# Stick-breaking heads taken in pairs with keys in chunks of 512, and a reordered expert loop

## The chip, the cores and the metric

One core of a Trainium2 chip runs the whole kernel. The metric is the device time in microseconds (us). Its engines are TensorE (PE, with weight loads as PEld), VectorE (DVE), ScalarE (ACT), GpSimd (POOL) and SyncE (SP); each runs its own program, and they meet only at semaphores.

## What is computed

An encoder block on 1024 tokens of width 1024, all in float32:

```python
h = rms_norm(x); q, k, v of both head groups = h @ w_in + b_in
# 8 stick-breaking heads of 64, no softmax; strict means key < query
log_1m  = where(strict, log_sigmoid(-z), 0)          # z = q k^T / 8
between = reversed cumsum of log_1m over the keys - log_1m
w       = where(strict, exp(log_sigmoid(z) + between), 0);  out = w @ v
# 8 sliding-window heads with sinks and a T5 bias, window 128
x = x + rms_norm-ed heads @ w_out + b_out
x = x + mixture of 32 experts, top 4 of each token, clamped SwiGLU, inner width 1024
out = rms_norm(x)
```

A query tile of 128 rows needs the keys up to its own last row, so tile i has i+1 key blocks of 128.

## The kernel before

The kernel has four stages: normalising and transposing x; the input projection, woven into the stick-breaking heads; the sliding-window heads, woven into the output projection, the router and the writing of slot records; and the expert loop. P is 128, S is 1024, NT is 8 and KT is 8.

**Input projection.** There are 18 chunks of 128 output columns. Each has two halves of 512 tokens, and each half is 24 matmuls in `project_steps` (line 773): three products of high and low float32r parts for each of 8 k. The first three chunks run alone; the other 15 are cut into pieces by `fill_end` and run between the steps of the stick-breaking heads, as work for PE while ACT and DVE work on a step. `project_steps` uses one PSUM bank, and ACT empties it in `projected` (line 1168).

**Stick-breaking heads.** A unit u is one head of one query tile with all its keys; there are 64, in four pairs of heads. On PE, iteration u is: `scores` of units ahead (q k^T in lines 826 and 828, the second adding the causal mask), the transposes of v halves that are due, the piece of projection, `turn(u)` (line 801: transposes the weights, 128 columns at a time, into PSUM banks 4 and 5 alternately, one group of up to 4 blocks a bank) and `values(u-1)` (line 853). Scores run up to three units ahead, or two where the unit ahead has over 4 blocks and so takes two of the four score banks 0 to 3. On ACT, iteration u is: `softplus_tail(u)` (abs, exp, ln: lines 1218 to 1220), `empty(u-2)` (copies the transposed weights out of PSUM, line 1190), `weights(u-1)` (exp, line 1227), the copies of v halves, and `projected`. On DVE, `stick(u)` is an elementwise step (line 1538), the running sum from the last key back to the first (line 1542) and the subtraction z - sum (line 1544); `keep_out` copies a finished tile.

**Expert loop.** An item is one expert with up to 192 tokens, the first 128 in the main part and the rest, if there are more than 128, as overflow; the loop runs over 33 items. An item's weights are 24 units of 128 x 1024: 16 for gate and up (`hidden`, line 1001) and 8 for down (`down`, line 1023), each six matmuls. ACT makes the high part of each unit (`high_part`, line 1357), DVE the low part (`low_part`, line 1799), in a ring of five slots, so a high part for unit u waits until PE has used unit u-5. Between them stand `room` (relu), `silu`, `clamp`, `hidden_out` (they give the activation of one half), `turn_hidden` on PE (line 1007, transposes that half) and `act_high_part` and `act_low_part`, which split it for `down`. For overflow tokens PE runs `over_hidden` (line 1035, in column tiles of 32 or 64 columns), `turn_over` and `over_out` (line 1052) behind branches on the token count. Near the end of an item PE transposes the gathered rows of the next one (`turn_rows`, line 969, and `turn_extra_rows`, line 977); ACT copies them (`x_high_part`, `extra_rows`, line 1340) and `expert_bias` of the next item waits for them.

SP loads weights and, once an item, its slot records: `load_slots` (line 500) issues eight small DMAs, two of them for row indices and gates of the tokens and six for the overflow in other layouts.

Of the kernel before, what the change touches and what calls it, by code (L numbers as in the profile page):

```python
# [7 lines left out]
ALU = mybir.AluOpType  # L8
# [8 lines left out]
P = 128  # L17
D = 1024
S = 1024
# [37 lines left out]
SLOT_LOADS = 16 * (2 + sum(PARTS))  # L57
# [14 lines left out]
def program(nc, x, attn_norm, w_in, b_in, sb_out_norm, sw_out_norm, sinks, rel_bias_table, w_out, b_out,  # L72
# [12 lines left out]
    with ExitStack() as ctx:  # L85
# [62 lines left out]
        tA = kb("tA", [P, 2, S], F32, 166)  # L148
        tB = kb("tB", [P, 2, S], F32, 174)
        wT = kb("wT", [P, 2, NT, P], F32, 182)  # L150
# [105 lines left out]
        d_slot = sem("d_slot")  # L256
# [51 lines left out]
        units = [(i, 2 * p + a, "sb") for p in range(PAIRS) for i in range(NT) for a in range(2)]  # L308
        SB = len(units)
        units += [(i, j, "sw") for i in range(NT) for j in range(BAND)]  # L310
# [10 lines left out]
        def blocks(u):  # L321
            i, _, kind = units[u]
            return i + 1 if kind == "sb" else 2 * min(i + 1, 2)

        z_bank, prev = [], []
        holder, nxt = [-1] * 4, 0
        for u in range(SB):
            wide = blocks(u) > 4
            if wide and nxt % 2:
                nxt += 1  # L330
            b = nxt % 4
            held = [b, b + 1] if wide else [b]
            z_bank.append(b)
            prev.append(max(holder[k] for k in held))
            for k in held:
                holder[k] = u
            nxt = b + len(held)
        prev += [holder[0], holder[1]] + list(range(SB, NU - 2))

        def z(u):  # L340
            n = blocks(u)
            if units[u][2] == "sw":
                return bank[:, u % 2, 0:n * P]
            if n > 4:
                return bank[:, z_bank[u]:z_bank[u] + 2, :].rearrange("p a b -> p (a b)")[:, 0:n * P]
            return bank[:, z_bank[u], 0:n * P]
# [3 lines left out]
        for p in range(PAIRS):  # L350
            begin = at_step
            for j in range(16):
                part = range(12) if j < 12 else range(12, 16)
                whole = sum(q // 2 + 1 for q in part)
                so_far = sum(q // 2 + 1 for q in part if q <= j)
                first, steps = (0, 3) if j < 12 else (3, AHEAD[p] - 3)
# [16 lines left out]
        def add_groups(key, n):  # L373
            first_group[key] = len(groups)
            for b in range(0, n, 4):
                groups.append((key, b, min(4, n - b)))
# [1550 lines left out]
```

## Time and profile before

| | |
|---|---|
| median of 3 runs | 2253.32 us (2247.72 to 2255.8) |
| the profiled execution: its time | 2252.55 us |
| its span | 2250.4 us |
| PE, DVE, ACT busy share of the span | 94%, 68%, 65% |
| stage of stick-breaking heads and input projection | from 76 to 472 us of the span |
| stage of sliding-window heads and output projection | 472 to 778 us |
| expert loop | 778 to 2212 us |

A busy PE is not a PE at its peak, since matmuls overlap in the records; the distance from one start to the next is what a matmul costs. PEclk is the granted clock, in tenths of 2.4 GHz in the page's slices and as a fraction in the windows. A number in square brackets behind a row of a timeline is the engine's idle time before it, with what ended it; "issue" is idle time that no wait explains.

### The profile page before, as it was taken

To read this page: it belongs to the slowest core of one execution; us is meant where nothing else is said; L and a number is where in the kernel's file an instruction comes from. 1 tells how busy PE (TensorE), PEld (TensorE's weight loads), DVE (VectorE), ACT (ScalarE), POOL (GpSimd) and SP (SyncE) were. 2 spreads that over 40 slices of the span, in tenths; PEclk is the share of its full clock that TensorE was granted. 3 is DMA by queue.
4 is the path that set the end of the run, shared out by engine and by line. 5 is a ranking of instruction groups with operands and counts; after the bars stand their busy time and mean duration, and the time that the engine had idled before them with its cause. 6 is when DMAs were issued, how large, how long until landed. Compare 5 with 4: busy or idle time off the path is not lost.

```text
span 2250.4 us, 37586 instructions
## 1 busy us (share of the span) xinstructions
PE 2108.3 (94%) x11367; PEld 1606.5 (71%) x11368; DVE 1521.1 (68%) x1908; ACT 1468.0 (65%) x1944; POOL 323.4 (14%) x327
## 2 busy tenths in 40 slices
PE   5999999999988499999999999999999999999997
PEld 4777777777766377878777777777776777676683
DVE  4355455553545678888888777787786688675585
ACT  4456565653332378888788687787785687675583
POOL 1000000001123211202011121111111121010022
PEclk9899999958989599999999999999999999999996
DMA  6300000110113789999899898899897899797694
GB/s 193 60 24 19 19 20 19 50 73 29 58 39 116 266 268 381 370 381 372 292 342 334 289 342 291 298 377 296 290 376 244 282 338 318 279 313 242 221 318 176
DMA packets 250409, 507.19 MB, mean 225 GB/s; under 512 B 44454, under 2 KB 62676, under 8 KB 250228
## 3 DMA queue, kind: packets, MB, share of 16 engines
q1 hardware_dynamic: 234724, 462.98, 58.4%
q0 software_dynamic: 15632, 43.53, 7.5%
q8 instruction: 31, 0.51, 0.1%
q14 instruction: 22, 0.18, 0.0%
HBM read 470.25 MB, written 38.54 MB: 226 GB/s over the span
## 4 chain that ended last, share of the span: by engine, by line
PE 71%; DVE 12%; issue 9%; ACT 4%; DMA 2%; POOL 1%; SPq 0%; DVEq 0%; ACTq 0%; POOLq 0%
PE bank L1001 23%; PE bank L1023 12%; PE bank L773 8%; PE bank L1035 6%; DVE w_low L1799 6%; PE bank L871 4%; PE bank L1052 3%; PE bank L826 2%; PE bank L853 2%; PE bank L801 2%; PE bank L816 2%; PE bank L842 2%; PE bank L1117 1%; PE bank L991 1%; DVE act_low L1813 1%
## 5 line engine op out<-in xcount | busy, mean ns | idle before, releaser
L1799 DVE TENSOR_TENSOR w_low<-gu_w,w_high 128x1024 fp32r<-128x1024 f32 x528 | 620.0, 1223 | 242.2 <-ACT w_high L1357 234.0
L1357 ACT CAST w_high<-gu_w 128x1024 fp32r<-128x1024 f32 x528 | 534.9, 1050 | 163.4 <-PE bank L1001 86.7
L1001 PE MATMUL bank<-w_high,x_high 128*128 128x512 f32 x1056 | 416.1, 394 | 3.0 <-DVE w_low L1799 3.0
L1001 PE MATMUL bank<-w_high,x_low 128*128 128x512 f32 x1056 | 413.9, 392 | 0.0
L1001 PE MATMUL bank<-w_low,x_high 128*128 128x512 f32 x1056 | 413.3, 391 | 0.0
L1799 DVE TENSOR_TENSOR w_low<-dn_w,w_high 128x1024 fp32r<-128x1024 f32 x264 | 315.1, 1225 | 19.5 <-ACT w_high L1357 13.2
L1357 ACT CAST w_high<-dn_w 128x1024 fp32r<-128x1024 f32 x264 | 270.8, 1050 | 23.1 <-PE bank L1001 13.4
L1023 PE MATMUL bank<-w_high,act_high 128*128 128x512 f32 x528 | 212.6, 403 | 23.9 <-DVE act_low L1813 23.9
L1001 PEld LDWEIGHTS bank<-w_high,x_high 128*128 128x128 f32 x1056 | 199.0, 188 | 46.6 <-DVE w_low L1799 3.8
L1001 PEld LDWEIGHTS bank<-w_high,x_low 128*128 128x128 f32 x1056 | 198.8, 188 | 42.8
L1001 PEld LDWEIGHTS bank<-w_low,x_high 128*128 128x128 f32 x1056 | 199.1, 189 | 42.1
L1023 PE MATMUL bank<-w_high,act_low 128*128 128x512 f32 x528 | 206.3, 391 | 0.0
L1023 PE MATMUL bank<-w_low,act_high 128*128 128x512 f32 x528 | 205.7, 390 | 0.0
L1023 PEld LDWEIGHTS bank<-w_high,act_high 128*128 128x128 f32 x528 | 99.0, 187 | 63.2 <-DVE w_low L1799 28.5
L677 POOL DMA_INDIRECT residual_rows<-y_sb,scat_idx x33 | 55.5, 1682 | 584.1 <-ACT y_sb L1365 316.4
L1035 PE MATMUL bank<-gu_w,xo 128*32 128x256 f32 (+1 forms) x1536 | 129.0, 415 | 0.0
L773 PE MATMUL bank<-hT_high,in_high 128*128 128x512 f32 x288 | 122.3, 425 | 1.2 <-DVEq L1521 0.9
L773 PE MATMUL bank<-hT_low,in_high 128*128 128x512 f32 x288 | 119.5, 415 | 0.0
L773 PE MATMUL bank<-hT_high,in_low 128*128 128x512 f32 x288 | 117.9, 409 | 0.0
L1023 PEld LDWEIGHTS bank<-w_high,act_low 128*128 128x128 f32 x528 | 99.1, 188 | 21.6
L1023 PEld LDWEIGHTS bank<-w_low,act_high 128*128 128x128 f32 x528 | 99.2, 188 | 18.8
L1538 DVE SCALAR_TENSOR_TENSOR tA<-bank,tA 128x128 f32<-128x128 f32 (+7 forms) x64 | 48.4, 756 | 90.6 <-ACT tA L1220 90.6
(223 smaller groups left out, 3136.7 us busy)
## 6 DMA issues: line engine op xcount, KB each, us to landing
gu_w<-in_w_gate_up SPq DMA_DIRECT2D x528, 512.0 KB, 11.3
dn_w<-in_w_down SPq DMA_DIRECT2D x132, 1024.0 KB, 18.4
w_st<-in_w_in SPq DMA_DIRECT2D x14, 512.0 KB, 4.8
xt<-in_x SPq DMA_DIRECT2D x8, 512.0 KB, 4.4
wo_sb<-in_w_out SPq DMA_DIRECT2D x2, 2048.0 KB, 9.7
x<-in_x SPq DMA_DIRECT2D x8, 512.0 KB, 4.2
residual_rows<-x SPq DMA_DIRECT2D x8, 512.0 KB, 2.7
h_rows<-h SPq DMA_DIRECT2D x8, 512.0 KB, 2.9
```

The lines of the kernel that those rows point to most:

```text
L677: pool.indirect_dma_start(acc_dram.rearrange("r (q d) -> (r q) d", q=parts), bass.IndirectOffsetOnAxis(ap=scat_idx[:, k:k + 1].bitcast(U32 ...
L773: mm = pe.matmul(bank[:, proj_bank(n), :], a, b[:, k, cols], start=(r == 0), stop=(r == HALF_STEPS - 1))
L801: mm = pe.transpose(bank[:, 4 + g % 2, P * (b % 4):P * (b % 4) + P], src[:, P * b:P * b + P], ident)
L816: mm = pe.matmul(out_z[:, n * a:n * a + n], qk_sw[rows, 2 * (h % 2) + a, i * P:i * P + P], qk_sw[rows, 4, k0:k0 + n], start=True, stop=True)
L871: mm = pe.matmul(bank[:, 2 + half, :], a, b[:, k, cols], start=first, stop=last)
L1001: mm = pe.matmul(bank[:, 2 * h + g, :], a[:, k, :], b, start=False, stop=last)
L1023: mm = pe.matmul(bank[:, 4 + half, :], a[:, j, :], b, start=first, stop=last)
L1035: mm = pe.matmul(over_view(parts)[m * q:m * q + m, h], lhs, rhs[:, :, w * q:w * q + w], start=(k < 0), stop=(k == KT - 1))
L1052: mm = pe.matmul(bank[m * q:m * q + m, 7, 0:n], overT[:, c0:c0 + m], dn_w[:, j, n * q:n * q + n], start=(j == 0), stop=(j == FT - 1))
L1357: act.copy(w_high[:, u % RING, :], src).then_inc(high_ready, 1)
L1538: chain(dve.scalar_tensor_tensor(ta, z(u), 0.0, ta, ALU.max, ALU.add))
L1799: dve.tensor_tensor(w_low[:, u % RING, :], raw, w_high[:, u % RING, :], ALU.subtract).then_inc(split_ready, 1)
```

## The change

In the stick-breaking heads a step is now one pair of heads with up to 512 keys. A tile with up to 4 blocks is one step; a tile with more is two steps, the later keys first (part 1), then the first 512 (part 0), whose running sum starts from the end of the other's. A pair has 12 steps, there are 48. Each step's scores are two matmuls next to each other, one on partitions 0 to 63 and one on 64 to 127, into two banks; each of the two pairs of banks holds one step, so scores run one step ahead for all. The weights stay in tA, not tB. The projection's pieces are dealt out anew. In the expert loop `turn_hidden(i, 1)` stands behind three down units, not four, with silu, hidden_out, act_high_part and act_low_part one unit earlier beside the high and low parts. The six overflow loads of slot records move from SP to ACT, inside the branch taken where the next item has over 128 tokens, with two value loads for every item in front of the branch.

```diff
+        units = [(i, p, part) for p in range(PAIRS) for i in range(NT) for part in ((1, 0) if i >= 4 else (0,))]
+        def keys_of(u):
+            i, _, part = units[u]
+            return (4, i - 3) if part else (0, min(i + 1, 4))
         def z(u):
+            if u < SB:
+                return bank[:, 2 * (u % 2):2 * (u % 2) + 2, 0:keys_of(u)[1] * P]
+            begin, work = at_step, [keys_of(PER * p + j)[1] + 1 for j in range(PER)]
+            if p == PAIRS - 1:
+                work[-1] = 0
+            for j in range(PER):
+                want = begin + 2 * HALF_STEPS * AHEAD[p] * sum(work[:j + 1]) // sum(work)
+                stop = min(want, (at_step // HALF_STEPS + 1) * HALF_STEPS) if j < PER - 2 else want
 # scores
-                for c0 in range(0, cols, 512):
-                    n = min(512, cols - c0)
-                    pe.matmul(out_z[:, c0:c0 + n], q[r0:r0 + HD, i * P:i * P + P],
-                              k[r0:r0 + HD, c0:c0 + n], start=True, stop=c0 + n < cols)
-                pe.matmul(out_z[:, P * i:P * i + P], ident_b[:], causal_b[:], start=False, stop=True).then_inc(z_ready, 1)
+                for a in range(2):
+                    rows = slice(HD * a, HD * a + HD)
+                    mm = pe.matmul(z(u)[:, a, :], qk_pair[rows, h % 2, 0, i * P:i * P + P],
+                                   qk_pair[rows, h % 2, 1, b0 * P:(b0 + n) * P], start=True, stop=not opens(u))
+                if opens(u):
+                    for a in range(2):
+                        mm = pe.matmul(z(u)[:, a, P * (n - 1):P * n], ident_b[:], causal_b[:], start=False, stop=True)
 # PE loop over units
-                reach = 1 if u >= SB else 3
-                while ahead < NU and ahead <= u + (2 if ahead < SB and blocks(ahead) > 4 else 1 if ahead > SB else reach):
+                while ahead < NU and ahead <= u + 1:
 # DVE stick
-                dve.tensor_tensor_scan(tb[:, ::-1], ta[:, ::-1], ta[:, ::-1], 0.0, ALU.add, ALU.max).then_inc(sum_done, 1)
+                for a in range(2):
+                    so_far = 0.0 if opens(u) else tB[:, (u - 1) % 2, a, 0:1]
+                    ins = dve.tensor_tensor_scan(tb[:, a, ::-1], ta[:, a, ::-1], ta[:, a, ::-1], so_far, ALU.add, ALU.max)
+                ins.then_inc(sum_done, 1)
 # PE expert loop
-                down(i, range(4))
+                down(i, range(3))
                 turn_hidden(i, 1)
+                down(i, range(3, 4))
 # ACT expert loop
                 room(i, 0)
-                high_part(i, range(12, 13))
                 silu(i, 0)
-                high_part(i, range(13, 17))
+                high_part(i, range(12, 17))
 ...
+                silu(i, 1)
                 high_part(i, range(20, 21))
-                silu(i, 1)
                 over_silu(i, n_tok)
-                high_part(i, range(21, 24))
+                high_part(i, range(21, 23))
                 act_high_part(i, 1)
+                high_part(i, range(23, 24))
                 over_turned(i, n_tok)
                 x_high_part(i + 1)
-                extra_rows(i + 1, n_next)
+                e = act.value_load(item_tab[0:1, bass.ds(i + 1, 1)], min_val=0, max_val=NE - 1)
+                first = act.value_load(item_tab[0:1, bass.ds(i + (2 * MAX_ITEMS + 1), 1)], min_val=0, max_val=SLOTS - ITEM)
+                act.wait_ge(d_over_slot, OVER_LOADS * i + OVER_LOADS)
+                act.sem_inc(act_passed, 1)
+                extra_rows(i + 1, n_next, e, first)
 # extra_rows
                 with act.If(n_tok > P):
+                    over_slots(n, e, first)      # six act.dma_start into slot_in
                     act.wait_ge(xo_psum, n + 1)
```

## Rows read from the trace of the kernel before

**Rows 1.** The page, parts 1 and 2: PE over the span; granted clock in 40 slices.
```profile
PE 2108.3 (94%) x11367; PEld 1606.5 (71%) x11368; DVE 1521.1 (68%) x1908; ACT 1468.0 (65%) x1944; POOL 323.4 (14%) x327
...
PEclk9899999958989599999999999999999999999996
```
**Rows 2.** Windows: stretch, its length, busy us (instructions) of PE, PEld, DVE, ACT, POOL, clock, DMA.
```profile
176.00:276.00 100.00, 95.86 (x488) 73.40 (x487) 52.09 (x60) 60.55 (x103) 0.00 (x0) 0.95 0.09 22
...
375.00:472.00 97.00, 95.18 (x478) 74.40 (x477) 50.26 (x66) 60.63 (x107) 0.00 (x0) 0.89 0.12 44
...
1200.00:2212.00 1012.00, 996.54 (x5844) 740.86 (x5842) 751.76 (x744) 735.79 (x822) 158.87 (x155) 1.00 0.87 297
```
**Rows 3.** Groups of instructions, 76 to 472 us, PE: busy us, mean ns of one.
```profile
L826 PE MATMUL bank<-qk_pair 64*128 64x512 f32 x96 | 54.1, 658 | 0.0
```
**Rows 4.** Timeline of one unit of 7 blocks: start, length, engine, line.
```profile
227.51 1.77 PE L826 MATMUL bank<-qk_pair 64*128 64x512 f32 x4
...
228.04 0.19 PEld L826 LDWEIGHTS bank<-qk_pair 64*128 64x128 f32 x1 [0.24 <-issue]
...
228.47 0.19 PEld L826 LDWEIGHTS bank<-qk_pair 64*128 64x128 f32 x1 [0.24 <-issue]
...
229.25 0.48 PE L773 MATMUL bank<-hT_high,in_high 128*128 128x512 f32 x1
...
229.80 0.39 PE L773 MATMUL bank<-hT_low,in_high 128*128 128x512 f32 x1
...
234.57 0.39 PE L773 MATMUL bank<-hT_low,in_high 128*128 128x512 f32 x1
```
**Rows 5.** Timeline, overflow matmuls in column tiles, four tiles in turn.
```profile
803.08 3.42 PE L1035 MATMUL bank<-gu_w,xo 128*32 128x256 f32 x60
```
**Rows 6.** Timeline of ACT and PE near the end of a pair.
```profile
238.36 0.84 ACT L1190 COPY wT<-bank 128x512 f32<-128x512 f32 x2
...
239.08 0.93 PE L801 MATMUL bank<-cst,v_t 128*128 128x128 f32 x4 [0.54 <-ACT wT L1190]
...
259.18 1.02 ACT L1218 ACTIVATE tA<-bank 128x1024 f32<-128x1024 f32 x1 [1.05 <-PE bank L828]
...
261.33 1.06 ACT L1220 ACTIVATE tA<-tA 128x1024 f32<-128x1024 f32 x1
```
**Rows 7.** Waits of PE, 76 to 472 us: total, times, longest.
```profile
PE bank L826 <- DVE tB L1544: 6.5, 3, 2.2
PE bank L801 <- ACT wT L1190: 4.7, 6, 1.0
```
**Rows 8.** Waits of PE, 778 to 2212 us.
```profile
PE bank L1023 <- DVE act_low L1813: 23.9, 28, 1.5
```
**Rows 9.** Timeline, end of an item without overflow, the next without too.
```profile
1004.75 1.28 ACT L1357 ACT_TABLE_LOAD   x1 [1.26 <-issue]
...
1007.13 3.85 DVE L1799 TENSOR_TENSOR w_low<-gu_w,w_high 128x1024 fp32r<-128x1024 f32 x3 [1.83 <-ACT w_high L1357]
...
1010.31 0.40 PE L1001 MATMUL bank<-w_high,x_high 128*128 128x512 f32 x1
```
**Rows 10.** Timeline, end of an item without overflow, the next with overflow.
```profile
1205.34 4.63 DVE L1799 TENSOR_TENSOR w_low<-gu_w,w_high 128x1024 fp32r<-128x1024 f32 x4 [2.50 <-ACT w_high L1357]
...
1207.83 0.40 PE L1001 MATMUL bank<-w_high,x_high 128*128 128x512 f32 x1
```
**Rows 11.** Timeline, end of an item with overflow, the next with overflow.
```profile
1251.14 3.50 DVE L1799 TENSOR_TENSOR w_low<-gu_w,w_high 128x1024 fp32r<-128x1024 f32 x3 [3.31 <-ACT w_high L1357]
...
1256.92 0.40 PE L1001 MATMUL bank<-w_low,x_high 128*128 128x512 f32 x1
```
**Rows 12.** Timeline of SP: the eight slot loads of an item, alone and beside weight loads.
```profile
1206.00 6.12 SPq L500 DMA_DIRECT2D slot_in<-slot_rows  x8
...
1306.76 4.78 SPq L500 DMA_DIRECT2D slot_in<-slot_rows  x8
```
**Rows 13.** Line 1340, the copy of overflow rows: one for each item with overflow.
```profile
L1340 ACT COPY xo<-bank x14: 586/586/620, 766.8 to 2062.4; 128x512 f32<-128x512 f32 x14
```

More of the change, by code:

```diff
@@ L319, in tile_at, with opens, closes, sizes @@
             return t if rest == 0 and 0 <= t < NT else None
[L321 to L338, printed above, removed]
-        def z(u):
[L341 to L346, printed above, removed]
+        def keys_of(u):
+            i, _, part = units[u]
+            return (4, i - 3) if part else (0, min(i + 1, 4))
+        def opens(u):
+            return units[u][2] == 1 or units[u][0] < 4
+        def closes(u):
+            return units[u][2] == 0
+        tile_end = [u for u in range(SB) if closes(u)]
+        def sizes(key):
+            if not isinstance(key, int):
+                return [4]
+            return [keys_of(key)[1]] * 2 if key < SB else [2 * min(units[key][0] + 1, 2)]
+        def z(u):
+            if u < SB:
+                return bank[:, 2 * (u % 2):2 * (u % 2) + 2, 0:keys_of(u)[1] * P]
+            return bank[:, u % 2, 0:sizes(u)[0] * P]
         HALF_STEPS = 3 * KT
@@ L350, in program @@
         for p in range(PAIRS):
[L351 to L356, printed above, removed]
-                want = begin + 2 * HALF_STEPS * first + 2 * HALF_STEPS * steps * so_far // whole
-                stop = min(want, (at_step // HALF_STEPS + 1) * HALF_STEPS) if j not in (11, 15) else want
-                halves_at[16 * p + j] = range(at_step // HALF_STEPS, stop // HALF_STEPS)
+            begin, work = at_step, [keys_of(PER * p + j)[1] + 1 for j in range(PER)]
[4 more added lines that the diff above has]
+                stop = min(want, (at_step // HALF_STEPS + 1) * HALF_STEPS) if j < PER - 2 else want
+                halves_at[PER * p + j] = range(at_step // HALF_STEPS, stop // HALF_STEPS)
                 at_step = stop
@@ L1173, in empty @@
             def empty(key):
-                n = blocks(key) if isinstance(key, int) else 4
-                for b in range(0, n, 4):
-                    g = first_group[key] + b // 4
-                    w = min(4, n - b)
+                for a, w in enumerate(sizes(key)):
+                    g = first_group[key] + a
                     act.wait_ge(wt_psum, g + 1)
@@ L1222, in weights @@
             def weights(u):
-                i, h, kind = units[u]
+                i, h, part = units[u]
                 act.wait_ge(logw_ready, u + 1)
-                if kind == "sb":
-                    a = tB[:, u % 2, 0:blocks(u) * P]
+                if u < SB:
+                    a = tA[:, u % 2, :, 0:keys_of(u)[1] * P]
                     act.activation(a, a, ACT.Exp).then_inc(w_ready, 1)
                 else:
-                    n = blocks(u) * P // 2
+                    n = sizes(u)[0] * P // 2
                     for k in range(2):
```

168 lines of the change are left out of this document (87 added, 81 removed).

## The prediction

> **What bounds the kernel now.** I read the page first: PE is busy for 94% of the span and no other engine passes 68% [rows 1], so the end is set by PE's work plus the holes in it. Then the windows by stage: in the stick-breaking stage PE is busy for over 95 of 100 us while ACT and DVE stand at 50 to 61 [rows 2], and in the expert loop for 996 of 1012 us. Then PE's own waits, by stage: in the stick-breaking stage the two that matter come to 11 us [rows 7] and with the small ones to about 15; in the expert loop there is one, for act_low, of 23.9 us [rows 8]. The clock is 0.89 to 0.95 in the stick-breaking stage and 1.00 in the expert loop [rows 2], so the first is not quite at the 2.4 GHz level and the second is. The sliding-window stage keeps its code, and I take it as unchanged. The reader should keep in mind that both changed stages are bound by PE with little reserve: a microsecond taken from PE's stream counts in full, and so does one by which ACT comes too late.
>
> **Scores in row tiles.** Each float32 score matmul leaves two records. The second and the third of a 7-block unit start 0.43 us apart [rows 4], both 512 wide or behind one of 512, and the group of 512 has 96 records [rows 3]. Per head the tiles have 128 x (1+...+8) = 4608 columns, for 8 heads 36864, which is 72 times 512, times two records, times 0.427: 61.5 us. The overhead of a unit is 229.25 - 227.51 = 1.74 us less 1.49 for its 896 columns: 0.25 us, for going into the 64-row shape, out of it and the mask. If two row tiles run side by side the stream costs half: -30.8 us. No row shows row tiles. The nearest is four column tiles in turn: 60 records of 256 float32 columns in 3.42 us, 0.057 each [rows 5], where one alone would need about 0.21 by the 0.427 above; so four run as one. Bounds: 0 (they queue) to -30.8; I take -30.8. Sixteen units fewer at 0.25, less 32 mask matmuls that now stand next to another, make about -3. Sum for PE's stream: **-34**. ACT and DVE save some fixed cost of 16 fewer instructions of each kind, which is worth nothing unless they bind.
>
> **One step ahead instead of two or three.** This is what I think decides the stage. In the new order PE issues scores(u+1) at the start of iteration u. ACT then has, in its program, softplus_tail(u+1), empty(u-1), weights(u), and only the last releases turn(u) on PE. For 1024 elements abs and exp and ln take 261.33 - 259.18 + 1.06 = 3.2 us, the two copies 0.84 and the exp 1.07 [rows 6]; with 0.2 until the scores have landed it is 5.3 us. Beside them PE has only the piece of projection: 21 steps from 229.80 to 234.57, 0.227 each [rows 4], so it takes 23 steps to cover a full step. Before, the scores were issued an iteration earlier and ACT ran softplus_tail(u+1) during turn and values; that is why rows 7 are small. The diff deals the 192 steps of a pair out as 8, 12, 4, 24, 16, 8, 24, 20, 4, 24, 28, 20, since a piece may not pass the end of a half. Scaling the ACT operations by width (0.21 us + 0.83 ns an element, which gives 1.06 for 1024) I get, for each of the 12 iterations, what ACT needs after the scores less what the piece covers. It is positive in six: 1.5, 0.9, 3.7 (the piece of 4 before a step of four blocks), 1.0, 1.5 and 4.1 (the other piece of 4): 12.8 us a pair, 12 in the first. The last pair, with 144 steps dealt as 6, 10, 8, 22, 2, 22, 2, 24, 14, 10, 24, 0, gives 19. Sum **+57**.
>
> A second wait comes with it. A v half is transposed on PE right behind the scores and ahead of the piece, and needs the PSUM bank that empty(u-1) empties, which on ACT now stands behind softplus_tail(u+1). Before it cost 0.54 us in the case shown, 4.7 over six [rows 6, 7]. Now it is 0.2 + 3.1 + 0.4 = 3.7 us for a full step, and nothing covers it, because the piece comes later. Of the eight halves in this stage six fall on full steps and two on narrow ones (about 2): **+26**. The old waits of about 15 go: **-14**. Both new waits are worked out and not seen; bounds are 30 and 110 us together for the 83.
>
> The clock: the two levels cost the stage something now (0.89 to 0.95). More holes should not raise it, fewer score matmuls neither. I leave it as it is, with 0 to +20 for the range.
>
> Stage: -34 + 57 + 26 - 14 = **+35** (from -25 to +75).
>
> The Trainium skill's page TensorEngine Tiling (Array Packing), PSUM Bottleneck, says that tiling speeds up TensorE but not the evacuation of PSUM, which can become the bound. It speaks against this part: by it the 31 us would be lost to ACT and DVE. The rows that bear on it are those of ACT above; no run here shows it yet, and my sum does not use it.
>
> **The turn behind three down units.** The wait of 23.9 us [rows 8] is PE standing in front of down unit 4 for act_low. Stepping through the items, it is about 1.5 us where neither this item nor the next has overflow (11 items), 0.7 where the next has (8), and small else. In the new order the transposes come 1.36 us (six steps) earlier and one down unit stands behind them, and act_high and act_low (0.6 + 0.7) are no longer queued behind the high and low parts of unit 23. So the wait goes: up to -23.9. Unit 23 itself is needed three units later. The earlier silus push unit 12 and unit 20 back by one operation, and these have over 1 us of reserve. Cost 0 there.
>
> **What is late next.** PE now reaches the next item 1.5 us earlier and needs its unit 0. ACT, behind x_high_part, has two value loads, a table load, the high part; DVE the low part. The low part of unit 0 ends at 1007.13 + 1.23 = 1008.4 and PE starts on it at 1010.31 [rows 9]: a reserve of 1.9 us. The change adds two value loads for every item; the two of before are the idle 1.26 us ahead of the table load [rows 9], so +1.27. Unit 0 is then late by 1.5 + 1.27 - 1.9 = 0.9, and of the 1.5 only 0.6 stays: 11 x -0.6 = **-7**.
>
> **Slot loads on ACT.** 14 items have overflow [rows 13]; for each ACT issues six DMAs in its own program, ahead of the copy xo and the next high part. SP needs 4.78 us for eight, 6.12 beside weight loads [rows 12]: 3.6 to 4.6 for six. No row shows an issue on ACT: bounds 0.05 us each (nothing but a queue entry) to 1.2 each (it waits for SP's in turn); I take SP's, since it is the same instruction. With the value loads ACT is 4.9 to 5.9 us later. The reserve where an item without overflow is followed by one with is 1207.83 - 1206.57 = 1.3 us [rows 10]. That makes +3.6 to +4.6, I take 4.0, for 8 items: **+32**. Where both have overflow, the reserve is 1256.7 - 1252.4 = 4.3 (PE's first matmul is 0.24 ahead of the one shown) [rows 11]: +0.6 for three items, none for the two longer ones: **+2**. Where only the first has, the reserve holds and the old wait of some 0.4 goes: **-2**. SP is rid of six issues an item; PE never waits for a weight load, so that gives nothing. POOL waits for the new semaphore only in scatter, long after it landed.
>
> The Trainium skill's page DMA: Bandwidth & Descriptors, Issuing engines are not separate DMA queues, says that spreading issues over engines saves only the issuing sequencer's time. It speaks against this part too: what is saved is SP's time, which is spare, and what is paid is ACT's. No run here shows the ACT side.
>
> Expert loop: -7 + 32 + 2 - 2 = **+25** (from -15 to +60).
>
> **Sum.** The profiled execution took 2252.55 us (2250.4 of span), 0.8 below the median. 2252.55 + 35 + 25 = 2312.6; against the median I say **2313 us**.
>
> **Rivals.**
> A. The waits in the stick-breaking stage do not come: ACT gets softplus_tail(u+1) under turn and values after all, or the pieces cover it. Place: PE in front of turn(u); it decides once ACT needs less than the piece, about 5.3 against 24 steps. The stage then gives -34 + 0, and with the expert loop as forecast 2252.5 - 34 + 25 = 2244. For it: ACT is busy for only 60 of 100 us. Against: its order is fixed, and those 40 us are idle just where PE does turn and values. Chance 0.09.
> B. The issues on ACT are nearly free. Then the expert loop is -7 - 8 x 0.7 (the reserve of 1.3 just about covers the value loads) - 2 = -14, total 2252.5 + 35 - 14 = 2274. For it: nothing on ACT waits for their data. Against: SP's rows. Chance 0.17.
> C. A and B together: 2252.5 - 34 - 14 = 2204, the case that ends on the other side; it needs ACT off PE's path in both stages. Chance 0.07.
> D. The row tiles queue: the 31 us stay, 2344. For it: nothing shows row tiles. Against: rows 5. Chance 0.12.
> E. ACT's issues wait for SP's, one to one with weight loads of about 1 us: 8 us more delay over 11 items at half of that, some +40: 2353. Chance 0.1.
> Forecast as above: 0.45.
>
> **How the numbers follow.** About 0.5% (11 us) is what a measurement can tell from no change. Faster by more: C, and just under half of A: 0.11. Within: the rest of A and the lower edge of B: 0.08. Slower: 0.81. For 8 in 10 I leave out C and part of A below, and the far ends of D and E above: 2250 to 2355.
>
> **What would show it.** Right: PE waits for line 1227 (exp) in front of the transposes in most iterations, up to 4 us for pieces of 4, and for the wT copies in front of v; records of the two score matmuls start within 0.02 us of each other; PE in the expert loop waits no longer for act_low but for w_low of unit 0, 4 us where the next item has overflow; six DMA issues of 0.5 us on ACT. Wrong: a stick-breaking stage under 396 us; score records 0.43 us apart throughout; PE without waits at the head of items. The forecast fails most easily at the 83 us of worked-out waits.

## The result, and the profile after

The changed kernel takes 2356.3 us (median of 4 runs, 2352.5 to 2361.7) against 2251.7 for the kernel before (4 runs): a ratio of 1.047, with a 95% interval from 1.044 to 1.050. It is slower, as forecast, but by 105 us and not by 60: 43 us above the forecast of 2313 and 1 us above the end of its range, 2355. The profiled execution has a span of 2360.1 us, 109.7 more than before, which is 50 more than the sum of 60; what follows is measured in profiled executions and accounts for these 50.

Parts 1 and 2 of the page of the kernel after, PE over the span and the granted clock in 40 slices, as [rows 1]:

```profile
PE 2133.7 (90%) x11367; PEld 1625.8 (69%) x11368; DVE 1519.5 (64%) x1908; ACT 1457.3 (62%) x1880; POOL 321.5 (14%) x327
...
PEclk9989898785899789999999999999999999999996
```

PE has the same number of instructions, its busy time has grown by 25 us, and its share has fallen from 94 to 90%. The third to the ninth digit of the clock are 8 9 8 9 8 7 8, where before the third to the eighth were all 9s.

Windows by stage (stretch, length, busy us of PE, PEld, DVE, ACT, POOL, granted clock, DMA). First the kernel before, from 76 us to its first sliding-window scores, and its expert loop; then the same two stretches of the kernel after:

```profile
76.00:454.00 378.00, 363.60 (x1792) 273.14 (x1792) 201.56 (x238) 229.73 (x396) 1.04 (x2) 0.94 0.11 33
...
773.00:2208.00 1435.00, 1411.14 (x8042) 1074.57 (x8043) 1114.09 (x1097) 1086.32 (x1206) 229.10 (x229) 1.00 0.90 310
```
```profile
76.00:526.00 450.00, 368.57 (x1833) 285.10 (x1832) 206.42 (x242) 225.44 (x337) 1.04 (x2) 0.86 0.07 20
...
843.00:2318.00 1475.00, 1433.12 (x8043) 1084.49 (x8044) 1113.57 (x1098) 1085.05 (x1206) 228.64 (x229) 0.98 0.87 301
```

The stick-breaking stage, measured so, is 72 us longer (450 for 378) and the loop 40 (1475 for 1435). The rest is within 3 us of before. The granted clock, third from the end of a row, is the column that the forecast had passed over: from 0.94 to 0.86 in the stage, from 1.00 to 0.98 in the loop. Since the clock has only its two levels of 1.2 and 2.4 GHz, 0.94 of 378 us means 45 us at half (twice 0.06 of 378; 47.5 in the trace's record of the clock) and 0.86 of 450 means 126.

Waits of PE in the kernel after (total, times, longest), from 76 to 581 us and then in the loop, as [rows 7, 8]:

```profile
PE bank L788 <- ACT tA L1219: 53.3, 25, 4.1
PE bank L788 <- ACT wT L1182: 27.3, 8, 3.9
```
```profile
PE bank L994 <- DVE w_low L1809: 39.9, 21, 4.0
PE bank L1016 <- DVE act_low L1823: 5.6, 11, 0.6
```

All four are where the forecast put them: the exp of the weights (tA, forecast 57), the copies in front of v halves (wT, forecast 26), unit 0 of an item (w_low, about 4 us where ACT had issued), and what is left of the 23.9 us for act_low.

What the forecast did not have is seen behind these waits. Timeline of the kernel after (start, length), the head of an item with overflow behind one without, as [rows 10]:

```profile
1274.78 3.32 ACTq L1336 DMA_DIRECT2D slot_in<-slot_rows  x6
...
1278.21 0.59 ACT L1344 COPY xo<-bank 128x512 f32<-128x512 f32 x1 [4.59 <-issue]
...
1283.76 0.79 PE L994 MATMUL bank<-w_high,x_high 128*128 128x512 f32 x1 [3.99 <-DVE w_low L1809]
...
1284.36 0.63 PE L994 MATMUL bank<-w_low,x_high 128*128 128x512 f32 x1
...
1284.78 0.63 PE L994 MATMUL bank<-w_high,x_low 128*128 128x512 f32 x1
```

ACT's six issues take 3.4 us, from 1274.78 to the copy at 1278.21, and with the value loads ACT is idle for 4.59; PE waits 3.99 us for unit 0. Then its matmuls come 0.42 us apart, where 512 columns take 0.23 in [rows 4]. That lasts until 1289.3. In the trace's record of the clock there are eight such stretches at half in the loop, 3.4 to 6.9 us long, each at the head of one of the eight items with overflow that follow one without: 48 us. With each goes a wait of PE of 3.99 to 4.01 us. The kernel before has none there.

In the stick-breaking stage it is the same. Timeline of PE in front of a v half of the kernel after:

```profile
387.95 1.08 PE L788 MATMUL bank<-cst,v_t 128*128 128x128 f32 x4 [3.75 <-ACT wT L1182]
...
389.26 0.63 PE L761 MATMUL bank<-hT_high,in_low 128*128 128x512 f32 x1
...
389.68 0.63 PE L761 MATMUL bank<-hT_low,in_high 128*128 128x512 f32 x1
...
391.74 0.39 PE L761 MATMUL bank<-hT_high,in_low 128*128 128x512 f32 x1
...
391.97 0.40 PE L761 MATMUL bank<-hT_low,in_high 128*128 128x512 f32 x1
```

A wait of 3.75 us, then projection steps 0.42 us apart, and 0.23 again from 391.7 on.

The row tiles do what they should. Timeline of the kernel after, scores of one full step, as the first line of [rows 4]:

```profile
396.58 1.13 PE L811 MATMUL bank<-qk_pair 64*128 64x512 f32 x4
```

Four records of 512 columns in 1.13 us (each float32 score matmul leaves two, and the two heads make four); the first records of the two heads start 7 ns apart, and so do their second ones, 0.53 us later.

### The profile page after: what moved, and what is told of

Its sections match the earlier page's. It is cut to its first block, busy times and chain, and to the rows that moved or that the text cites. A ratio compares the mean times of both kernels' runs of the same rounds, so it can differ in the third digit from the quotient of the medians.

```text
span 2360.1 us, 37433 instructions
## 1 busy us (share of the span) xinstructions
PE 2133.7 (90%) x11367; PEld 1625.8 (69%) x11368; DVE 1519.5 (64%) x1908; ACT 1457.3 (62%) x1880; POOL 321.5 (14%) x327
## 4 chain that ended last, share of the span: by engine, by line
PE 78%; ACT 6%; issue 5%; DVE 4%; ACTq 4%; DMA 2%; POOL 1%; SPq 0%; DVEq 0%; POOLq 0%
PE bank L994 31%; PE bank L1016 10%; PE bank L761 7%; PE bank L1028 6%; PE bank L865 4%; PE bank L846 3%; PE bank L788 3%; PE bank L1045 2%; PE bank L811 2%; ACTq L1336 2%; PE bank L802 2%; DVE w_low L1809 1%; PE bank L830 1%; ACT tA L1211 1%; ACT tA L1210 1%
## 5 line engine op out<-in xcount | busy, mean ns | idle before, releaser
L1362 ACT CAST w_high<-gu_w 128x1024 fp32r<-128x1024 f32 x528 | 526.9, 1049 | 119.5 <-PE bank L994 92.4
L994 PE MATMUL bank<-w_high,x_high 128*128 128x512 f32 x1056 | 426.7, 404 | 40.1 <-DVE w_low L1809 39.9
L994 PE MATMUL bank<-w_high,x_low 128*128 128x512 f32 x1056 | 420.2, 398 | 0.0
L994 PE MATMUL bank<-w_low,x_high 128*128 128x512 f32 x1056 | 420.0, 398 | 0.0
L1210 ACT ACTIVATE tA<-bank 128x1024 f32<-128x1024 f32 (+3 forms) x48 | 38.9, 811 | 153.9 <-PE bank L815 118.5
L1548 DVE SCALAR_TENSOR_TENSOR tA<-bank,tA 128x1024 f32<-128x1024 f32 (+3 forms) x48 | 46.0, 958 | 128.3 <-ACT tA L1212 128.2
```

What stands on the lines that cost most here:

```text
L994: mm = pe.matmul(bank[:, 2 * h + g, :], a[:, k, :], b, start=False, stop=last)
L1210: chain(act.activation(a, z(u), ACT.Abs))
L1362: act.copy(w_high[:, u % RING, :], src).then_inc(high_ready, 1)
```

## The experiments

The theory by now: the waits are as forecast, and the missing 50 us (109.7 of span less 60) are matmuls at the 1.2 GHz level behind those of about 4 us. The main rival: the change costs something else that was not counted (row tiles that save little, the new place of the turn), and the clock is a side effect without a price.

**1. Slot loads back on SP.** The kernel after, less the part on ACT, here its main lines:

```diff
-                e = act.value_load(item_tab[0:1, bass.ds(i + 1, 1)], min_val=0, max_val=NE - 1)
-                first = act.value_load(item_tab[0:1, bass.ds(i + (2 * MAX_ITEMS + 1), 1)], min_val=0, max_val=SLOTS - ITEM)
...
                 with act.If(n_tok > P):
-                    over_slots(n, e, first)
```

> The kernel after, with the six overflow loads of slot records back on SP, unconditional, and without ACT's two value loads; the stick-breaking heads in pairs and the turn behind three down units stay. Theory: the expert loop of the kernel after pays for ACT's six issues twice, once as a wait of PE for w_low of about 3.7 us where an item without overflow is followed by one with (8 times), and once because the granted clock falls to the 1.2 GHz level for about 3 to 7 us behind it. Without the issues both go, and of the loop there stays the gain of the earlier turn: up to the 23.9 us of the act_low wait of before. So the loop gives -10 to -23, the stick-breaking stage stays +67, the sliding-window stage +2: 2297 to 2312 us, the middle 2302; no stretch at half clock in the loop. Rival: the loop is slower for the turn's new place itself (unit 23's high part behind act_high), then this kernel stays above 2330.

Measured: 2299.3 us, 57 less than after, 1.022 (1.020 to 1.025) of before. The loop, by windows of this kernel:

```profile
843.00:2256.00 1413.00, 1408.24 (x8043) 1072.11 (x8043) 1109.13 (x1097) 1085.67 (x1205) 226.94 (x229) 1.00 0.91 315
```

The clock is back at 1.00 and the loop at 1413, 62 less than after. Of the stage nothing changed. So 57 us of the 105 belong to the six DMA issues of an item with overflow and the two value loads of every item, of which the waits explain 37 (39.9 against 2.8 in this kernel, the first item's).

**2. The turn alone**, on the kernel before:

```diff
-                down(i, range(4))
+                down(i, range(3))
                 turn_hidden(i, 1)
+                down(i, range(3, 4))
```
(and silu, hidden_out, act_high and act_low one unit earlier on ACT and DVE, as in the change)

> The kernel before with one part of the change alone: the turn behind three down units, with silu, hidden_out, act_high and act_low one unit earlier. Theory: the wait for act_low (23.9 us in 28 waits) goes, and unit 0 of the next item has a reserve of 1.9 us that takes the 1.5 us by which PE comes earlier, since the two value loads are not there: 2229 us, between 2225 and 2240, with the rest of a wait for unit 0 in the items followed by overflow (reserve 1.3). Rival: what is won ahead of unit 4 of down is lost in front of unit 0 of the next item, and the time stays within 5 us of before, 2252.

Measured: 2229.5 us, 0.991 (0.989 to 0.993): the turn is worth 21 us. Waits of PE in the loop of this kernel:

```profile
PE bank L1023 <- DVE act_low L1814: 4.8, 11, 0.5
PE bank L1001 <- DVE w_low L1800: 2.8, 1, 2.8
```

The 23.9 us of [rows 8] went to 4.8, and nothing came up in front of unit 0, whose 2.8 us (3.0 before) are those of the first item.

**3. The slot loads alone**, on the kernel before, with the value loads ahead of them as in the change:

```diff
+                    over_slots(n, e, first)
                     act.wait_ge(xo_psum, n + 1)
```

> The kernel before with the slot loads alone: six overflow loads on ACT in the branch, two value loads for every item. Theory: 8 items without overflow followed by one with get a wait for w_low of about 3 us (4.4 of issues, plus 1.3 for the value loads, less the reserve of 1.3 and what the act_low wait gives), and each is followed by 3 to 7 us at the 1.2 GHz level, which costs half of that: 8 x (3 to 4 + 1.5 to 3.5) = 36 to 60 us, 2288 to 2312, the middle 2298. With the delay alone and the clock unchanged it is 8 x 3.7 = 30: 2282. With issues that cost nothing it is 2252 to 2256.

Measured: 2290.4 us, +40, 1.018 (1.015 to 1.020). Waits of PE in its loop, and the loop's window:

```profile
PE bank L996 <- DVE w_low L1812: 31.1, 12, 3.9
PE bank L1018 <- DVE act_low L1826: 23.6, 28, 1.5
```
```profile
769.00:2246.00 1477.00, 1426.18 (x8044) 1082.44 (x8042) 1112.45 (x1097) 1081.16 (x1206) 226.99 (x229) 0.99 0.86 300
```

The delay alone gives 28 (31.1 less 3.0). The other 12 fit the half clock, which has 33 us here against 6. The same loads cost 57 in the kernel after, where the turn has moved: there PE waits for unit 0 in 21 items, not 12, and for 37 us more, not 28. The two parts of the change draw on the same reserve: ahead of unit 0 PE used to come later, because it had stood up to 1.5 us in front of down unit 4. In front of the eight items it now waits 4.0 us and here 3.2 to 3.6.

**4. Copies ahead of the softplus.** The kernel after with one exchange in ACT's loop:

```diff
             for u in range(SB + 2):
-                if u < SB:
-                    softplus_tail(u)
                 if u >= 2:
                     empty(u - 2)
+                if u < SB:
+                    softplus_tail(u)
```

> The kernel after with one exchange on ACT in the stick-breaking heads: empty(u-2) ahead of softplus_tail(u), so that the copies out of banks 4 and 5 no longer stand behind abs, exp and ln of the next step. Theory: PE's wait for these copies in front of the v halves (27.3 us in 8 waits) shrinks to under 5, and the 24 waits for exp(weights) shorten or stay (51.8), since the copies stood between ln and exp before: weights(u-1) now follows softplus_tail(u) directly, 0.85 earlier each, while softplus_tail starts no later where ACT is waiting for scores. With them goes part of the half clock behind the eight v waits, 3 us each at half cost. Stage 25 + 10 to 20 + 8 to 12 less: 2290 to 2315, the middle 2305. Rival: the new place makes softplus_tail late (the copies wait for turn(u-2)), and the exp waits grow by what the v waits give back: within 8 us of after, 2356.

Measured: 2295.1 us, 61 less than after, 1.020 (1.018 to 1.022) of before: inside the range, and a little more than the 43 to 57 us of the sum in it. Waits of PE in its stage, and the stage's window:

```profile
PE bank L788 <- ACT tA L1219: 40.4, 22, 3.2
...
PE bank L788 <- ACT wT L1182: 1.8, 5, 0.6
```
```profile
76.00:462.00 386.00, 342.81 (x1836) 265.08 (x1834) 205.83 (x242) 228.32 (x337) 1.04 (x2) 0.92 0.09 23
```

The waits give 38 (25 for v, 13 for the exp). The clock went from 0.86 of 450 to 0.92 of 386, from 126 us at half to 62 (58 in the record of the clock). Half clock costs nothing where PE waits anyway; of the part in PE's busy time 111 us became 56, worth 27. The stage is 64 shorter. So an exchange of two statements, which removes no instruction, gives back most of what the stage had lost.

**5. The row tiles taken away.** The kernel after with both score matmuls on partitions 0 to 63. The second head's own scores are left out; it gets the first head's, in as many instructions of the same size:

```diff
-                    rows = slice(HD * a, HD * a + HD)
+                    rows = slice(0, HD)
```

> The kernel after with both score matmuls of a step on partitions 0 to 63, so that the second head's scores are computed from the first head's q and k (its output is another for that reason); number and size of all instructions stay. In the trace of after the two stand side by side: records of the two 7 ns apart, two passes of 512 columns in 0.43 us each. Theory: the row tiles save the 30.8 us that the prediction counts for them, and nothing swallows them, since PE's stream sets the end in the long pieces and the scores lie on the chain of ACT in the short ones; with the part that runs at the 1.2 GHz level a few more. 2356 + 31 to 38: 2387 to 2394, records of the two 0.43 us apart. Rival, the one of the evacuation: ACT sets the pace of the stage and absorbs part, then less than +20, 2356 to 2376.

Measured: 2396.4 us, 40 more than after (31 between the profiled executions), 1.067 (1.063 to 1.071) of before. Timeline of a full step's scores in this kernel:

```profile
394.88 1.98 PE L811 MATMUL bank<-qk_pair 64*128 64x512 f32 x4
```

1.98 us for the four records and not 1.13, a difference of two starts of 0.43 each. The span from 76 us to the first output projection grew by 35, of which 5 is half of the 11 us more at half clock that its record of the clock has. What is left, 30, agrees with the 30.8 of the forecast. The rival that ACT and DVE swallow it is out, here: with both idle for half of the stage, there was nothing to swallow it.

**6. PE kept busy at the heads of items.** The kernel after, with

```diff
                 down(i, range(FT - 1, FT))
+                with pe.If(n_tok > P):
+                    pe.nop()
+                with pe.Else():
+                    with pe.If(n_next > P):
+                        for _ in range(5):
+                            pe.matmul(bank[:, 6, 0:3 * P], ident, cst[:, 0:3 * P], start=True, stop=True)
```

> The kernel after with five more matmuls on PE at the end of each item without overflow that is followed by one with, into a bank that nobody reads then: constants times constants, 384 float32 columns each, about 3.2 us together. They stand in the time in which PE waits for w_low of unit 0 anyway (8 waits of about 4 us). Nothing else changes, ACT and DVE come as late as before. Theory of the clock: it is the idle stretch that makes the granted clock fall to half for the 3 to 7 us after it (about 48 us in 8 stretches, which cost 24); with PE busy there the clock stays at 1.00 and the 24 us come back: 2332, between 2328 and 2340, the eight items 3 us shorter each. Rival: the slow matmuls behind the wait have another cause (the transfers, the weight loads, the new rows) or the clock falls anyhow: 2356 to 2365.

Measured: 2344.0 us, 12 less than after, 1.041 (1.038 to 1.043) of before, 4 above the end of the range; by the traces the loop is 17 shorter. Timeline of PE in the same place as above, and the loop's window:

```profile
1280.31 3.39 PE L1105 MATMUL bank<-cst 128*128 128x384 f32 x10
...
1284.96 0.50 PE L994 MATMUL bank<-w_high,x_high 128*128 128x512 f32 x1 [0.80 <-DVE w_low L1819]
1285.30 0.39 PE L994 MATMUL bank<-w_low,x_high 128*128 128x512 f32 x1
1285.53 0.40 PE L994 MATMUL bank<-w_high,x_low 128*128 128x512 f32 x1
```
```profile
846.00:2304.00 1458.00, 1441.96 (x8125) 1086.01 (x8126) 1109.49 (x1097) 1081.93 (x1206) 230.99 (x229) 1.00 0.87 304
```

With more work on PE the kernel is faster. ACT and DVE deliver unit 0 as late as before, the matmuls behind it come 0.23 us apart, and none of the eight stretches is left. So the idle stretch is the cause of the slow matmuls. The size was below the forecast of 24, for which I had halved all 48 us; a part of most stretches lies inside the wait (the one shown begins at 1282.5, PE at 1283.76) and costs nothing, 10 us in all. Without it there are about 38, worth 19.

**7. Experiments 1 and 4 together.**

> The kernel after with two of its parts changed: the slot loads back on SP and ACT's copies out of banks 4 and 5 ahead of the softplus. The two touch different stages, so their gains should add: 57 for the slot loads and 61 for the copies give 2356 - 118 = 2238. Range 2232 to 2245. If one eats into the other (a clock that depends on what lies in the other stage), it is above 2245.

Measured: 2237.5 us, 0.994 (0.992 to 0.996) of before: the two add to within 1 us. This is the whole change with two things put right, faster than before, though still slower than experiment 2, which has only the turn.

**8. Pieces of projection by need.** As 7, and

```diff
-            begin, work = at_step, [keys_of(PER * p + j)[1] + 1 for j in range(PER)]
...
+            deal = (10, 14, 24, 9, 15, 11, 13, 24, 24, 24, 16, 8) if p < PAIRS - 1 else (
+                10, 14, 15, 9, 14, 10, 13, 11, 12, 12, 24, 0)
+                stop = at_step + deal[j]
```

> As the kernel with slot loads back and copies first, and the projection dealt out by what ACT needs in each iteration, by hand: 10, 14, 24, 9, 15, 11, 13, 24, 24, 24, 16, 8 steps instead of 8, 12, 4, 24, 16, 8, 24, 20, 4, 24, 28, 20 in the first three pairs, and 10, 14, 15, 9, 14, 10, 13, 11, 12, 12, 24, 0 in the last. Same work in other places. Theory: the exp waits left (40.4 us in 22) come from pieces too short to cover ACT's work on a step; by what the short pieces showed, a full step needs 18 to 20 steps of projection beside it. The two pieces of 4 a pair (3.2 us each) go, some 4 us a pair stay in small waits, the last pair keeps about 10 as its 144 steps do not suffice. Waits 40 to about 20, and some of the half clock behind them: 2238 - 20 to -30 = 2208 to 2222. Rival: what counts is the sum of ACT's work, not its place, then the waits only move and it stays at 2238.

Measured: 2184.9 us, 52 less than 7 and 0.972 (0.969 to 0.975) of before. It is faster than both kernels and 23 us under the lower end of the range. The wait and the stage:

```profile
PE bank L791 <- ACT tA L1222: 16.1, 25, 1.8
```
```profile
76.00:410.00 334.00, 317.39 (x1833) 244.39 (x1832) 205.27 (x242) 228.42 (x338) 1.04 (x2) 1.00 0.10 26
```

The waits fell by about 23 (38.9 to 16.1 up to the same point), as expected. The stage fell by 52 (386 to 334), because its clock is 1.00 throughout: all of experiment 7's half clock is gone (58 us, 56 of them in PE's busy time, worth 28), not just that behind the longest waits.

**9. PE kept busy in the waits of the stick-breaking stage.** The kernel after, with `busy(count)` in front of v halves and before the last step of short pieces:

```diff
+                def busy(count, fresh):
+                    for _ in range(count):
+                        pe.matmul(bank[0:64, 7, 0:3 * P], cst[0:64, 64:128], cst[0:64, 0:3 * P], start=fresh, stop=fresh)
```

> The kernel after with PE kept busy in the waits of the stick-breaking stage: matmuls of 384 float32 columns of constants (0.64 us each at full clock), five in front of a v half where the next step is full and two where it isn't, and one to six before the last projection step of a short piece, as many as fit into the wait seen there (1.5, 0.9, 3.7, 0.9, 1.5 and 4.0 us in a pair). They add zero to a bank or are overwritten. ACT and DVE come as late as before; the waits for them shrink by what is put in. Theory of the clock: the stage has 180 us at the 1.2 GHz level against 101 before, because of its idle stretches, a part of which lies in the waits themselves; with PE busy this falls to about 100 and 20 to 35 us come back, less some 5 us where a filler runs over: 2356 - 25 = 2331, range 2320 to 2345. Rival: the half clock comes from something else in the stage (the float32 transposes, the scores side by side), then 180 us stay and the time is 2356 to 2366.

Measured: 2316.4 us, 40 less than after, 1.029 (1.026 to 1.033) of before, and 4 us under the lower end of the range. (The 180 and 101 us named there run up to the first output projection, the 126 and 45 above to the first sliding-window scores.) Timeline of PE in front of a v half, and the stage:

```profile
359.56 3.06 PE L937 MATMUL bank<-cst 64*64 64x384 f32 x9
...
363.01 0.63 PE L788 MATMUL bank<-cst,v_t 128*128 128x128 f32 x4 [0.39 <-ACT wT L1193]
...
363.70 0.39 PE L761 MATMUL bank<-hT_high,in_low 128*128 128x512 f32 x1
363.93 0.39 PE L761 MATMUL bank<-hT_low,in_high 128*128 128x512 f32 x1
```
```profile
76.00:480.00 404.00, 394.99 (x2051) 272.85 (x2049) 206.11 (x242) 227.66 (x338) 1.04 (x2) 1.00 0.08 21
```

Some 110 matmuls of no use more, and the stage is 46 us shorter than in the kernel after, 404 for 450. The clock is 1.00, and the projection behind the v half runs at 0.23 us a step at once. PE's idle time fell from 81 us to 9, and the filling took about what the waits had taken (109 matmuls of about 0.65 us), so these 46 us are the price of the half clock, for the stage.

**10. Scores earlier.** As 8, and in PE's loop

```diff
                 turn(u)
+                if ahead == u + 2 and ahead < SB and ahead % PER:
+                    scores(ahead)
+                    ahead += 1
                 if u >= 1:
                     values(u - 1)
```

> The kernel with longer pieces (2185), and in the stick-breaking stage the scores of step u+2 issued right behind turn(u), ahead of values(u-1), in place of the start of iteration u+1; the banks are free then, since exp(u) followed the subtraction that reads them last. So values(u-1) and the v halves stand between scores and the wait, beside ACT's work, for steps that close a tile up to 1.7 us. Theory: of the 17.6 us in 26 exp waits about half go, with a little of the half clock (51 us now): 2185 - 10 to -15 = 2170 to 2176, range 2163 to 2182. Rival: ACT's order is the limit (copies of u-1, softplus of u+1, exp of u with no gap), then scores that are there earlier change nothing: 2183 to 2187.

Measured: 2189.2 us, 0.972 (0.969 to 0.975) of before, no different from 8 (2183.5 to 2192.8 against 2183.9 to 2192.8). The expectation, 2182 at most, failed. Waits of ACT in the stage, kernel 8 first and then this one:

```profile
ACT wT L1185 <- PE bank L849: 40.9, 14, 4.3
ACT tA L1213 <- PE bank L818: 18.6, 21, 2.3
...
ACT tA L1213 <- PE bank L814: 10.5, 16, 1.7
```
```profile
ACT wT L1188 <- PE bank L849: 54.0, 14, 5.2
...
ACT tA L1216 <- PE bank L814: 6.1, 15, 1.0
...
ACT tA L1216 <- PE bank L818: 4.7, 6, 1.1
```

ACT's wait for scores went from 29 to 11 us, but its wait for values(u-1), which must have read the buffer wT before the copies may write it, from 41 to 54. The values stand behind the scores now, and the copies stand ahead of the softplus on ACT. What one gained the other lost.

**11. Slot loads on ACT, later.** The kernel after, with the same six DMAs and two value loads for the item that runs, in its middle; `over_slots` issues two DMAs in a branch:

```diff
-                high_part(i, range(4, 12))
+                high_part(i, range(4, 7))
+                e = act.value_load(item_tab[0:1, bass.ds(i, 1)], min_val=0, max_val=NE - 1)
+                first = act.value_load(item_tab[0:1, bass.ds(i + 2 * MAX_ITEMS, 1)], min_val=0, max_val=SLOTS - ITEM)
+                over_slots(i, n_tok, e, first, 0)
+                high_part(i, range(7, 10))
+                over_slots(i, n_tok, e, first, 2)
```

> The kernel after with its slot loads still on ACT, six DMAs and two value loads, but for the item that runs, in the middle of it: the value loads behind high part 6, two DMAs each behind high parts 6, 9 and 14, each pair in a branch of its own, where the next item's first high parts don't wait behind them. Theory: the price of the issues is their place. In the middle of an item the ring of five slots gives ACT some reserve, and 1.3 us at a time fit into it; the waits at the heads of items (36 us) and the half clock behind them (20) go: 2299 as with the loads on SP, up to 2312 for what does not fit. Rival: it is the amount, since ACT has no reserve in an item either; then 14 items x (3.6 + 1.2) - 36 and the value loads of 19 items more: above 2330.

Measured: 2298.3 us, 58 less than after, 1.020 (1.017 to 1.024) of before: the same as with the loads on SP (2299.3). Waits of PE in its loop:

```profile
PE bank L1016 <- DVE act_low L1830: 6.2, 11, 0.6
PE bank L994 <- DVE w_low L1816: 2.8, 1, 2.8
```

ACT and its issues in the middle of an item of this kernel:

```profile
1275.13 1.04 ACT L1363 CAST w_high<-gu_w 128x1024 fp32r<-128x1024 f32 x1
1275.41 0.33 ACTq L1337 DMA_DIRECT2D slot_in<-slot_rows  x1
1276.08 2.19 ACT L1363 CAST w_high<-gu_w 128x1024 fp32r<-128x1024 f32 x2
```

This issue lies beside a running cast, and the next cast follows without a gap. Two issues between two casts have some 0.85 us of idle ACT beside them, and PE waits no longer for it. So in this place the issues have no price that the time shows; they have one where the next item's first high parts queue behind them.

## Why the prediction was wrong in size

**What held.** The scores in row tiles: -30.8 forecast for the stream, 30 by experiment 5. The exp waits: 57 forecast, 53.3 measured, and place by place too; in the second pair PE waited 1.4, 0.7, 3.6, 0, 0.7, 1.4 and 3.9 us in front of the turns behind the pieces of 8, 12, 4, 24, 16, 8 and 4 steps, against 1.5, 0.9, 3.7, 1.0, 1.5 and 4.1 for the six. The v halves: 26 forecast, 27.3 measured. The turn: up to 23.9 for the wait, of which 18 went in the kernel after and 19 in experiment 2, where all of it reached the end (21 us). The wait at the heads of the eight items with overflow: 4.0 forecast, 3.99 to 4.01 measured; six issues 3.4 us against 3.6 to 4.6. The 0.9 us in front of 11 other items was too high: the twelve other waits for w_low behind the first item's have 0.2 to 0.5 each. The new waits, none of which the trace of before could show, came within a few us of their size. They followed from the fixed order on ACT and its durations.

**The step that failed.** It is the paragraph on the clock: "More holes should not raise it, fewer score matmuls neither. I leave it as it is, with 0 to +20 for the range." In the stage the windows above show it. PE's idle time (the length less its busy time) rose from 14 to 81 us, 67 more, where the waits of the forecast come to 57 + 26 - 14 = 69. Its busy time rose by 5, where the forecast has -34 for fewer and shorter matmuls. So the +37 that are missing (72 measured against the +35 of the sum, and beyond the +20 that the range allowed) are not waits but slower matmuls. Of the 126 us at half 111 lie in PE's busy time by the record of the clock, against 43 in the kernel before; at half price the 68 more are worth 34. Experiment 9 bears that out: it took away all but 3 us of half clock, also that of the kind which the kernel before has, and won 46. For the expert loop the forecast had no clock term at all, because its clock was 1.00 throughout [rows 2]; there the waits changed by +37 and -18, that is +19 against the +25 of the sum, and the clock brought about 20 (17 in the loop's length by experiment 6, 12 in the time). The two terms, 37 and 20, are the missing 50, less the 6 by which the loop's waits were over-estimated.

The rows to see it by stood in the forecast. [rows 2] has 0.89 in a stage without long waits, and I had just worked out more than a dozen waits of close to 4 us for it and eight for the loop. The Trainium skill's page TensorE: Matmul & The Clock Gate, HAM oscillation — how this bites in real kernels, says that idle gaps of PE throttle the clock, and prices them: throttled time times one half. By that rule the sum would have had a term for each long wait. Experiments 6 and 9 agree with it as an upper bound, once the part of the throttled time that falls into a wait is left out: 17 us back for half of 38, and 46 for half of the 108 that went.

**The rivals.** A and B (waits that do not come, issues that are free), and with them C, are out by the rows above. B was right in one thing: the issues are free in another place (experiment 11). D (the row tiles queue) would have given 2344 and E (issues that wait for SP's) 2353, near the measured time, and both are wrong: experiment 5, and six issues in 3.4 us while SP issued two weight loads (from 1273.44, for 2.91 us). The number alone would have spoken for either of them.

**Two rules weighed there.** The Trainium skill's page TensorEngine Tiling (Array Packing), PSUM Bottleneck, says that the evacuation of PSUM may become the bound. In experiment 5 the stream's gain came through in full; what bound instead was the order on ACT (experiment 4). The Trainium skill's page DMA: Bandwidth & Descriptors, Issuing engines are not separate DMA queues, says that only the sequencer's time of starting a DMA is saved, which is usually small beside the DMA itself. The runs agree as to the gain (2298.3 us with six issues an item off SP in experiment 11, 2299.3 with them on SP in experiment 1), and experiment 1 shows the price on the other engine, 57 us.

**What stays open.** The kernel before has 45 us at half clock in this stage without waits of 4 us. Timeline and windows of PE in the kernel before, around one such stretch:

```profile
155.82 0.93 PE L801 MATMUL bank<-cst,tB 128*128 128x128 f32 x7
156.58 1.45 PE L853 MATMUL bank<-v_pair,wT 128*128 128x64 f32 x12
157.96 1.98 PE L826 MATMUL bank<-qk_pair 64*128 64x512 f32 x4
```
```profile
155.00:161.00 6.00, 5.10 (x29) 3.43 (x27) 4.98 (x5) 4.88 (x7) 0.00 (x0) 0.98 0.00 0
161.00:167.00 6.00, 4.72 (x12) 3.67 (x13) 2.64 (x3) 2.27 (x3) 0.00 (x0) 0.50 0.02 4
```

Ahead of the fall PE did transposes, values of 64 columns and scores on 64 rows, back to back; the clock fell at 160.8 us, 0.6 us into a wait of 2.2. In experiment 8, with waits of at most 1.8 us and these same kinds of matmul dealt out otherwise, the clock never fell in the stage, though PE was idle for 17 us there and for 14 before. So it is not the sum of the idle time. Whether it is the kind of work, its length in one go or the single wait that comes with it was not separated. Nor was the last part of experiment 6: 17 us came back where 19 were to be had.

## What to carry to other kernels

When a change puts waits of several microseconds into a PE that was never idle, price each with the clock: here the loss was the wait plus half of the slow time behind it (38 us for eight waits), so 4 us cost about 6. Before giving up such a change, look at what the late engine does just ahead of the wait: an order exchanged on ACT (61 us), a slot load put where nobody queues behind it (58) and filler work dealt by what the other engine needs rather than in proportion (52) were each worth more than the row tiles (31). Experiment 8, which has the first and the third and leaves the slot loads on SP, made 2356 into 2185. And two parts of a change that draw on one reserve, as the earlier turn and the slot loads did (40 alone, 57 together), are to be costed together.

## What the runs showed of the hardware

PE doing useless matmuls in its waits made the kernel faster, by 12 us in the loop and 40 in the stage. Two float32 row tiles of 64 rows ran side by side (records 7 ns apart, both heads' 512 columns in 1.13 us and not 1.98). Six DMA issues in a row on ACT kept it from its own instructions for 3.43 us, 0.57 each, about as much as one on SP [rows 12], with nothing waiting for the data; one beside a running cast took 0.33 us and left no gap (experiment 11).
